# The first norm postponed behind three chunks, and one modulation piece moved, in a three-layer fp32 transformer kernel

## The reference

```python
def rmsnorm(x, g):
    y = xf * lax.rsqrt(jnp.mean(xf * xf, axis=-1, keepdims=True) + EPS) * g
h = rmsnorm(x, attn_pre_norm[l])
proj = h @ w_in[l]
...
qm = rmsnorm(c_q, q_latent_norm) @ w_uq       # c_q, c_kv, k_rope, keys, queries, values: columns of proj
kv = rmsnorm(c_kv, kv_latent_norm) @ w_ukv
```

## Time and profile before

| | us |
|---|---|
| median of 3 runs (range) | 1070.65 (1069.55 to 1073.02) |
| the profiled execution | 1071.52 |
| its span in the profile | 1069.7 |
| PE busy in the span | 1038.4 (97%) |
| DVE, ACT, POOL busy | 809.5, 589.0, 153.1 |
| granted TensorE clock, mean | 0.993 of 2.4 GHz |

### The profile page before, as it was taken

One profiled execution on the slowest core, in us unless ns is written; L12 is line 12 of the kernel. 1 busy time (PEld: TensorE's weight loads), 2 busy tenths in 40 slices (PEclk: granted clock), 3 DMA queues, 4 the chain that ended last, 5 costly groups with the idle time before them and its releaser, 6 DMA issues.

```text
span 1069.7 us, 20330 instructions
## 1 busy us (share of the span) xinstructions
PE 1038.4 (97%) x7901; PEld 986.4 (92%) x7901; DVE 809.5 (76%) x1392; ACT 589.0 (55%) x1015; POOL 153.1 (14%) x162
## 2 busy tenths in 40 slices
PE   7999999999999999999999999999999999999997
PEld 6987798999888997899999999988899999999997
DVE  5867689999997987588999788885558567675453
ACT  6686467666536675675444445533466456544442
POOL 0000033333201200023111011200000113111010
PEclk8999999999999999999999999999999999999999
DMA  9642245777695443257998788454343536774540
GB/s 365 242 158 80 80 150 201 291 287 261 257 397 233 161 154 120 89 196 281 373 350 326 279 318 305 161 193 159 119 138 140 210 143 215 251 301 137 169 166 39
DMA packets 33684, 227.25 MB, mean 212 GB/s; under 512 B 3747, under 2 KB 4044, under 8 KB 9932
## 3 DMA queue, kind: packets, MB, share of 16 engines
q1 hardware_dynamic: 33164, 223.63, 56.6%
q0 software_dynamic: 448, 2.63, 0.6%
HBM read 225.19 MB, written 2.63 MB: 213 GB/s over the span
## 4 chain that ended last, share of the span: by engine, by line
PE 72%; DVE 18%; ACT 5%; issue 3%; DMA 1%; DVEq 0%; POOL 0%; ACTq 0%; SPq 0%
PE psum L1385 17%; PE psum L1387 17%; PE psum L1386 17%; DVE w_lo L2091 7%; DVE arena L2195 4%; PE psum L1750 3%; PE psum L1752 3%; PE psum L1751 3%; PE psum L1450 2%; PE psum L1453 2%; PE psum L1452 2%; ACT w_hi L762 2%; DVE arena L2348 1%; DVE h_lo L2356 1%; DVE hid_lo L2176 1%
## 5 line engine op out<-in xcount | busy, mean ns | idle before, releaser
L2091 DVE TENSOR_TENSOR w_lo<-raw,w_hi 128x1024 fp32r<-128x1024 f32 (+1 forms) x342 | 390.9, 1165 | 155.0 <-ACT w_hi L762 147.8
L762 ACT ACTIVATE w_hi<-raw 128x1024 fp32r<-128x1024 f32 (+1 forms) x342 | 335.7, 997 | 217.1 <-PE psum L1387 161.0
L1385 PE MATMUL psum<-h_hi,w_hi 128*128 128x256 f32 (+1 forms) x1144 | 327.8, 287 | 10.2 <-DVE w_lo L2091 4.1
L1386 PE MATMUL psum<-h_lo,w_hi 128*128 128x256 f32 (+1 forms) x1144 | 322.2, 282 | 0.0
L1387 PE MATMUL psum<-h_hi,w_lo 128*128 128x256 f32 (+1 forms) x1144 | 320.9, 280 | 0.0
L1385 PE MATMUL psum<-hid_hi,w_hi 128*128 128x256 f32 (+1 forms) x952 | 271.5, 285 | 1.8 <-DVE w_lo L2091 1.5
L1387 PE MATMUL psum<-hid_hi,w_lo 128*128 128x256 f32 (+1 forms) x952 | 269.3, 283 | 0.0
L1386 PE MATMUL psum<-hid_lo,w_hi 128*128 128x256 f32 (+1 forms) x952 | 269.2, 283 | 0.0
L1385 PEld LDWEIGHTS psum<-h_hi,w_hi 128*128 128x128 f32 x1144 | 215.3, 188 | 15.2 <-DVE w_lo L2091 6.5
L1386 PEld LDWEIGHTS psum<-h_lo,w_hi 128*128 128x128 f32 x1144 | 216.3, 189 | 0.7 <-issue 0.7
L1387 PEld LDWEIGHTS psum<-h_hi,w_lo 128*128 128x128 f32 x1144 | 216.4, 189 | 0.0
(11 more groups left out here) (266 smaller groups left out, 1183.6 us busy)
## 6 DMA issues: line engine op xcount, KB each, us to landing
arena<-in_ada SPq DMA_DIRECT2D x48, 1024.0 KB, 6.3
raw<-in_gu SPq DMA_DIRECT2D x44, 1024.0 KB, 6.4
raw<-in_ret_in SPq DMA_DIRECT2D x24, 1024.0 KB, 4.7
raw<-in_up SPq DMA_DIRECT2D x22, 1024.0 KB, 4.9
raw<-in_dn SPq DMA_DIRECT2D x32, 704.0 KB, 4.2
raw<-in_qkv SPq DMA_DIRECT2D x12, 1024.0 KB, 5.4
raw<-in_down SPq DMA_DIRECT2D x11, 1024.0 KB, 7.5
raw<-in_ret_o SPq DMA_DIRECT2D x8, 1024.0 KB, 4.8
```

Source lines behind the costliest of these rows:

```text
L762: nc.scalar.activation(w_hi[chunk % SPLIT_SLOTS][:, a:b], raw[chunk % RAW_SLOTS][:, a:b], ACT.Copy)\
L1385: nc.tensor.matmul(out, w[0], hc, start=start, stop=False, skip_group_check=True)
L1386: nc.tensor.matmul(out, w[0], lc, start=False, stop=False, skip_group_check=True)
L2091: tt(w_lo[s][:, a:b], raw[chunk % RAW_SLOTS][:, a:b], w_hi[s][:, a:b].bitcast(F32), ALU.subtract)\
```

## The change

Three things.

1. The norm is postponed for LAT0, LAT1 and KA. They multiply x times its gain (`Z_PRE`, in the unused end of `hid_hi`, `hid_lo`), made by ACT and DVE straight from x. When the three leave their banks, DVE multiplies them with 1/rms (`leave_scaled`), which ACT has copied to SBUF (`rbc_pre`). QA0 is the first chunk on the normed h, whose eight tiles are made meanwhile. The sums and the spread of the norm stand inside LAT0 and LAT1. LAT0 is ordered by output half; its weights come in two DMAs; `ident` and `onehot` are loaded behind LAT1, tab1 behind QA0. 34 fillers instead of 16 stand ahead of it, none later in the norm.
2. One modulation piece leaves w_in (at QA0) and goes to up's 21st chunk (number 20), where pieces 19, 20 and 21 now follow each other.
3. The rounding of the latents stands behind the first scores and exponentials, the split of the values (ROWS1) ahead of both, and QA0's bank is emptied before the rounding.

On PE, the head of the program before; `busy` is the filler, `tra`/`sco` banks show as psum.

```diff
 ADA_PIECES = 24
-ADA_STEPS = [("w_in", 10, lambda c: int(c in (KA, QA0))), ("up", 22, lambda c: int(c >= 7 and c % 2)),
+ADA_STEPS = [("w_in", 10, lambda c: int(c == KA)), ("up", 22, lambda c: int(c >= 7 and c % 2 or c == 20)),
...
+        Z_PRE = (hid_hi[:, (FT - DT) * S:], hid_lo[:, (FT - DT) * S:])
+        rbc_pre = a1["pT"][:, 0:S]
...
             for k in (0, DT // 2):
                 cut = slice(k * S, (k + DT // 2) * S)
                 sp.dma_start(x[:, cut], dram["x"][:, cut]).then_inc(x_in[2 * k // DT], 16)
-            sp.dma_start(cols[:, :], dram["cols"]).then_inc(cols_in, 16)
-            sp.dma_start(onehot, dram["onehot"]).then_inc(onehot_in, 16)
-            sp.dma_start(ident[:, :], dram["ident"]).then_inc(ident_in, 16)
+                if k == 0:
+                    sp.dma_start(cols[:, :], dram["cols"]).then_inc(cols_in, 16)
...
                     src = dram[ph.name][bass.ds(step.n(lambda c: c * P), P), 0:n]
+                    if chunk == 0:
+                        sp.dma_start(raw[0][:, 0:n // 2], src[:, 0:n // 2]).then_inc(first_in, 16)
+                        sp.dma_start(raw[0][:, n // 2:n], src[:, n // 2:n]).then_inc(raw_in[0], 16)
+                        return
                     sp.dma_start(raw[slot][:, 0:n], src).then_inc(raw_in[slot], 16)
...
                     load(step)
                     if ph.name == "w_in" and step.j == 1:
+                        sp.dma_start(ident[:, :], dram["ident"]).then_inc(ident_in, 16)
+                        sp.dma_start(onehot, dram["onehot"]).then_inc(onehot_in, 16)
                         sp.dma_start(cond_silu, dram["cond"]).then_inc(cond_in, 16)
-                    if ph.name == "w_in" and step.j == 2:
+                    if ph.name == "w_in" and step.j == 3:
                         sp.dma_start(arena[:, TAB1_AT:TAB1_AT + dram["tab1"].shape[1]], dram["tab1"]).then_inc(tab1_in, 16)
...
-                act.wait_ge(raw_in[chunk % RAW_SLOTS], at(lambda k: 16 * (k // RAW_SLOTS + 1)))
+                if chunk or ahead != 0:
+                    act.wait_ge(raw_in[chunk % RAW_SLOTS], at(lambda k: 16 * (k // RAW_SLOTS + 1)))
                 for half, (a, b) in enumerate(of.halves(c)):
                     if ahead in (0, 1) and half != ahead:
                         continue
+                    if chunk == 0 and half == 0:
+                        act.wait_ge(first_in, 16)
...
-            for k in range(0, DT, 2):
+            act.wait_ge(cols_in, 16)
+            for k in range(DT):
                 if k % 4 == 0:
                     act.wait_ge(x_in[k // 4], 16)
+                cut = slice(k * S, (k + 1) * S)
+                nc.scalar.activation(Z_PRE[0][:, cut], x[:, cut], ACT.Identity, scale=col("pre", k)).then_inc(pre_hi, 1)
+                if k == 5:
+                    hi(0, ahead=0)
+            hi(0, ahead=1)
+            for k in range(0, DT, 2):
                 square(PRE, k, 2)
+            hi(LAT1)
             act.wait_ge(band_ps, 1)
             nc.scalar.activation(band, tra[0][0:8, 0:BAND], ACT.Copy).then_inc(band_ready, 1)
-            warm_root(PRE)
-            hi(0)
-            root(PRE)
-            round_h(PRE)
-            hi(LAT1)
             act.wait_ge(cond_in, 16)
             nc.scalar.activation(cond_silu, cond_silu, ACT.Silu).then_inc(cond_ready, 1)
+            root(PRE)
+            hi(KA)
+            act.wait_ge(rbc_ready, nth(PRE))
+            nc.scalar.activation(rbc_pre, spread_bank(PRE, 0), ACT.Copy).then_inc(pre_rbc, 1)
+            for k in range(DT):
+                round_tile(PRE, k)
+                if k in (1, 2):
+                    hi(QA0, ahead=k - 1)
+                if k == 3:
+                    act.wait_ge(lin_free[0], 1)
+                    act.wait_ge(lin_free[1], 1)
+                    square(LATENT, 0, 3)
+                if k == 6:
+                    root(LATENT)
+                    hi(ROWS0)
...
-            leave_features(LAT0, a1["lat"][:, 0:512])
-            hi(KA)
-            act.wait_ge(half_done, 2 * (LAT1 + 1))
-            nc.scalar.activation(a1["kr"], lin[1][:, S:2 * S], ACT.Copy)
-            leave(nc.scalar.activation(a1["lat"][:, 512:768], lin[1][:, 0:S], ACT.Copy), UNIT_OF[LAT1])
-            act.wait_ge(lin_free[0], 1)
-            act.wait_ge(lin_free[1], 1)
-            square(LATENT, 0, 3)
-            hi(QA0)
-            leave_features(KA, a1["ka"])
-            root(LATENT)
-            hi(ROWS0)
             nc.scalar.activation(warm[:, LATENT:LATENT + 1], ones[:, 0:1], ACT.Exp)
-            round_h(LATENT)
             leave_features(QA0, a1["qa"][:, 0:512], qscale)
             hi(ROWS1)
             exp_pair(0)
+            round_h(LATENT)
...
             hi(MLA)
             act.wait_ge(v_rows, 1)
+            act.wait_ge(h_tiles, tiles_before(GROUP))
             leave_rows(0)
...
             pe.wait_ge(busy_ready, 1)
-            keep_busy(16)
+            keep_busy(34)
             pe.wait_ge(cols_in, 16)
-            pe.wait_ge(onehot_in, 16)
-            nc.tensor.matmul(tra[0][0:8, 0:BAND], col("rel", 0, 8, BUCKETS + 1), onehot, start=True, stop=True).then_inc(band_ps, 1)
             pe.wait_ge(ones_filled, 1)
-            norm(PRE, 0, 8, 4)
+            def bias_band():
+                pe.wait_ge(onehot_in, 16)
+                nc.tensor.matmul(tra[0][0:8, 0:BAND], col("rel", 0, 8, BUCKETS + 1), onehot, start=True, stop=True).then_inc(band_ps, 1)
...
-                if first_tiles is not None:
+                if first_tiles is not None and by_tile:
                     order.sort(key=lambda o: o[1])
...
             ph = PH["w_in"]
-            features(ph, LAT0, bank_free(0), 2, DT, first_tiles=(h_tiles, 0))
-            features(ph, LAT1, bank_free(1), 2, DT)
+            features(ph, LAT0, bank_free(0), 2, DT, Z_PRE, first_tiles=(pre_tiles, 0), hooks={9: bias_band, 14: lambda: sums(PRE)}, by_tile=False)
+            features(ph, LAT1, bank_free(1), 2, DT, Z_PRE, hooks={8: lambda: spread(PRE)})
...
-            features(ph, KA, bank_free(2), 1, DT, hooks={4: rotate_keys})
+            features(ph, KA, bank_free(2), 1, DT, Z_PRE, hooks={4: rotate_keys})
             sums(LATENT)
-            features(ph, QA0, bank_free(3), 2, DT, hooks={11: lambda: spread(LATENT)})
+            features(ph, QA0, bank_free(3), 2, DT, first_tiles=(h_tiles, 0), hooks={11: lambda: spread(LATENT)})
...
             dve.wait_ge(cols_in, 16)
-            dve.wait_ge(ident_in, 16)
             dve.wait_ge(x_in[0], 16)
-            dve.wait_ge(x_in[1], 16)
+            for k in range(DT):
+                if k == 4:
+                    dve.wait_ge(x_in[1], 16)
+                cut = slice(k * S, (k + 1) * S)
+                dve.wait_ge(pre_hi, k + 1)
+                stt(Z_PRE[1][:, cut], x[:, cut], col("pre", k), Z_PRE[0][:, cut].bitcast(F32), ALU.mult, ALU.subtract).then_inc(pre_tiles, 1)
+                if k == 5:
+                    lo(0, ahead=0)
+            lo(0, ahead=1)
...
-            norm_h(PRE, lambda: lo(0))
+            lo(LAT1)
+            dve.wait_ge(ident_in, 16)
+            rstd(PRE)
+            lo(KA)
+            dve.wait_ge(cond_ready, 1)
+            pieces("w_in", Step(KA))
...
-            lo(LAT1)
-            lo(KA)
-            dve.wait_ge(cond_ready, 1)
-            pieces("w_in", Step(KA))
-            lo(QA0)
-            rstd(LATENT)
+            def leave_scaled(c, *todo):
+                dve.wait_ge(half_done, 2 * (c + 1))
+                for to, at in todo:
+                    n = to.shape[1] // S
+                    ins = tt(v3(to, n), v3(lin[UNIT_OF[c] % 2][:, at:at + n * S], n), over(rbc_pre, n), ALU.mult)
+                leave(ins, UNIT_OF[c])
+            dve.wait_ge(pre_rbc, 1)
+            leave_scaled(LAT0, (a1["lat"][:, 0:512], 0))
+            def scale_pre(k):
+                cut = slice(k * S, (k + 1) * S)
+                stt(e0["y"][:, cut], x[:, cut], col("pre", k), rbc_pre, ALU.mult, ALU.mult).then_inc(t_ready, 1)
+            scale_pre(0)
+            for k in range(DT):
+                if k + 1 < DT:
+                    scale_pre(k + 1)
+                cut = slice(k * S, (k + 1) * S)
+                dve.wait_ge(hh_ready, k + 1)
+                tt(hl[:, cut], e0["y"][:, cut], hh[:, cut].bitcast(F32), ALU.subtract).then_inc(h_tiles, 1)
+                if k == 1:
+                    leave_scaled(LAT1, (a1["lat"][:, 512:768], 0), (a1["kr"], S))
+                if k in (2, 3):
+                    lo(QA0, ahead=k - 2)
+                if k == 4:
+                    leave_scaled(KA, (a1["ka"], 0))
+                if k == 5:
+                    rstd(LATENT)
             lo(ROWS0)
             dve.wait_ge(tab1_in, 16)
             rotary(0, a1["kr"], a1["cos"], a1["sin"], 1)
+            lo(ROWS1)
+            dve.wait_ge(bias_in, 16)
+            score_pair(0)
             tiles_of(LATENT)
-            pieces("w_in", Step(QA0))
-            dve.wait_ge(bias_in, 16)
```

(2 more changed lines are left out.)

5 lines of the change are left out of this document (3 added, 2 removed).

## The result

The changed kernel took **1075.52 us** (median of 14 runs, 1072.60 to 1078.34), the kernel before 1072.99 (14 runs, 1069.55 to 1074.29): ratio **1.0027, 95% interval 1.0017 to 1.0037**. Forecast were 1069.0 and 1066.0 to 1072.4. So it is slower, by 2.5 us (the medians) to 2.9 us (the ratio), where 1.6 us of gain were forecast; only rival 1 had that size, by a mechanism that the trace does not show. The profiled execution took 1073.82 us, its span is 1071.8 (before 1071.52 and 1069.7).

What follows compares the result with a forecast made beforehand. PE was taken as full almost everywhere, so only its waits could be won. Start -3.5 and end of up +1.9 gave -1.6 on the profiled 1071.52: 1069.9, less 0.87 for the median, 1069.0 us; range 1066.0 to 1072.4.

Steps and rivals of the forecast that it cites:

- rival 1: End of up: down's four loads share the rings, chunk 0 lands at 276.3; net +2.7, 1073.4 us; chance 0.09.
- the first half of LAT0's weights lands at 8.5: Start: landing reckoned at the transfers' early rate; PE to start LAT0 at 11.0 instead of 17.14.
- If LAT0 runs at 1.2 GHz: Start: a low clock in LAT0 takes up to 4.6 us more, all but 1.9 hidden; none was counted.
- the band copy until 15.8: Start, ACT's list: the band copy follows LAT1's halves (15.4), ahead of Silu and its table, until 18.1.
- VectorE's list of 16.1 us as the bound: Start: DVE's queue binds from 20.9, eighth tile of h at 37.0; gain at the start 3.5 us.
- stood in DVE's shadow before: w_in: the piece that left (2.5 us of DVE, 1 MB of DMA) brings nothing of its own.
- SyncE's queue at the end of up: Piece 21's load waits for piece 19; down's first three chunks queue behind it, 12 us later.
- Its price, 1.9 us: Down's start: PE waits for the last taps from 279.3 to 281.2, 1.9 us; bounds 0.8 and 3.0.
- (2): End of up: the load is hidden, the piece costs 0 to 0.8 us; net -3.1, 1067.5 us; chance 0.12.
- (3): Start: DVE is quicker, gain 5 us; net -3.1, 1067.5 us; chance 0.09.
- (4): Start: the bias lands at 44.4, wanted at 41.8; 2.6 us lost, net +1.0, 1071.7 us; chance 0.09.
- (5): Start: a switch of ACT's tables costs twice its row, root 2.6 us later; net +1.0, 1071.7 us; chance 0.04.

Runs made afterwards that it cites:

- columns last: Changed kernel with its extra piece at up's chunk 8, plus the columns' transfer moved behind both halves of x; one profile, shift at 62 us -1.55.
- 52 fillers: Changed kernel with its extra piece at up's chunk 8, plus 52 fillers instead of 34; one profile, shift at 62 us -2.57.
- copied last: Changed kernel with its extra piece at up's chunk 8, plus ScalarE's band copy moved behind the root; one profile, shift at 62 us -1.55.
- the clock kept up and the band first: Changed kernel with extra piece at down's chunk 5, band's matmul and copy early, 52 fillers; ratio to before 0.9983, shift at 62 us -2.76.
- band first: Changed kernel with extra piece at up's chunk 8, band's matmul ahead of LAT0 and its copy ahead of the squares; ratio to before 0.9985.
- the piece alone: Kernel before with one edit: the piece that stood at QA0 is done at up's chunk 20; ratio to before 1.0044.
- load behind again: Second profile of the changed kernel with piece 21's load moved behind down's chunks 0 to 2; shift at 338 us +1.79.
- both pieces early with 52 fillers: The both pieces early kernel with 52 fillers instead of 34; ratio to before 1.0021.
- piece at chunk 8: Changed kernel with the extra piece at up's chunk 8 instead of 20; ratio to before 1.0005.
- both pieces early: Changed kernel with band's matmul and copy early, first piece ahead of the norm's mean, second where the first stood, eight in up; ratio to before 1.0017.

## Why the prediction was wrong, step by step

PE's large waits stood where the forecast had them, at both places; three terms of the sum were wrong. A lower clock behind an idle PE was put at nothing, twice: 1.5 us at the start and 1.7 at the end of `up`. The loads at the start delayed the root by 1.4 us, and the wait at `down` was 3.3 us and not 1.9.

- *Loads at the start* ("the first half of LAT0's weights lands at 8.5"): it landed at 10.05. x's second half kept ScalarE waiting until 8.77. This step is 1.6 us late: LAT0 at 12.62, not 11.0. It is half of why the root was late (1.4 of 2.9 us). I had divided bytes by 0.41 MB/us; with the columns between the halves of x the rate from 5 to 10 us was 344 GB/s, with the columns last 398.
- *"If LAT0 runs at 1.2 GHz ... I take none of it"*: **this is the choice that failed.** The clock did fall, behind an idle time of 3.97 us, and LAT0 took 1.5 us longer for it (7.5 us from its start to the sums against 6.0 with 52 fillers), near the 1.9 us that I had worked out as a bound and then put at nothing. It was not hidden, since LAT0's slow part delays the band's product inside it, for which ScalarE waits ahead of the root, and not only LAT1's end, which I had looked at. That is the other half.
- *"the band copy until 15.8"*: I had set it by ScalarE's own list, and forgot that it waits for a matmul behind nine of LAT0's blocks. It stood at 18.36 to 18.84. At full clock the wait is not there (52 fillers), so this miss and the one above are one and the same 1.54 us. Shown by three runs: copied first, copied last, or with PE quicker, the root comes 0.9 to 1.4 us earlier.
- *VectorE's list of 16.1 us as the bound*: right. From KA's split at 23.95 to the eighth tile of h it ran 15.9 us with one gap of 0.27, and PE's waits of 0.75 and 1.10 us were where I had put 1.0 and 1.3; the two small ones in QA0 did not come. It started 3 us later than forecast, and that is the whole of the missing gain: 3.5 forecast, 0.5 seen. With the clock kept up and the band first 2.8 were reached. What is left there is argued, not tested: the later loads and Sqrt's table, then the last step before the root (20.23).
- *The piece in w_in "stood in DVE's shadow before"*: nearly. Taken away from the kernel before, the shift at 62 us is -0.67 in one trace and +0.25 in another. Of these -0.21 and +0.40 stand already at the 5th rounding, by earlier or later loads, so the piece itself was worth some 0.5 and 0.15 us.
- *SyncE's queue at the end of up*: the mechanism was right. Loads at 252.01 and 263.33, down's chunk 0 landing at 271.42 (forecast 272.0), one wait of PE for L2439 in down's first chunk. That the landing fits so well is in part luck: the load left at 263.71, 1.4 us earlier than the 265.1 by which I had reckoned, and took 7.7 us instead of 6.9.
- *Its price, 1.9 us*: mis-sized. The taps ended at 281.67 (forecast 281.2; VectorE was half a microsecond ahead of my list until piece 21, which took 3.7 us and not 2.6), PE was there at 278.7 and not 279.3 (it was ahead of before), so it waited 3.04, and 0.25 for `w_lo` before; and **the wait took the clock with it, 1.7 us**, which I had put at nothing. My upper bound of 3.0 just covers the wait, and not its price. Nothing gave it back by 435 us: +3.93 at 338 and there.
- *Rivals*: down's chunks landed neither together (1) nor in time (2); VectorE was not quicker than its list (3); in the changed kernel nothing waited for the bias (4); the table switches (5) were as the row said.
- *The median as the profiled time less 0.87*: in 14 runs the median of before was 1072.99, not 1070.65 as in the first three. The level of my forecast was 2.3 us too low by that alone; the ratio, which is not touched by it, is 1.0027 where 0.9985 was forecast.

## What to carry to other kernels

A wait of the engine that is full costs its length and, where the granted clock falls behind it, more: 1.7 us here, in three of four traces with a wait of 1.6 to 3.0 us at that place. Price each new wait with the clock, and look at what the slowed work releases. When an item moves along a fixed order, check three queues for it: the engine's that does the work, the one that issues its load (what stands behind that load?), and the transfers' own room (which is argued here, not shown). To learn what one part of a change is worth, compare two kernels that differ in it alone, at a place next to it; the start looked like 0.5 us against the kernel before and like nothing against the kernel without the piece. A filler count is worth a test by itself whenever the first useful matmul moves.

## What the runs showed of the hardware

At a granted clock of 1.00, and with PE busy without a gap, the number of matmuls in a window still differs between executions and changes within one. Two windows, 600 to 640 and 960 to 1040 us, of the kernel before, the changed kernel and the piece alone:

```profile
600.00:640.00 40.00, 40.00 (x335) 40.00 (x335) 34.33 (x57) 18.72 (x29) 3.53 (x3) 1.00 0.86 319
960.00:1040.00 80.00, 80.00 (x679) 80.00 (x678) 39.27 (x48) 35.76 (x54) 8.71 (x11) 1.00 0.51 170
```

```profile
600.00:640.00 40.00, 40.00 (x340) 40.00 (x339) 33.71 (x56) 20.25 (x32) 2.57 (x3) 1.00 0.82 307
960.00:1040.00 80.00, 80.00 (x679) 80.00 (x678) 38.83 (x48) 36.05 (x54) 9.12 (x11) 1.00 0.48 163
```

```profile
600.00:640.00 40.00, 40.00 (x340) 40.00 (x339) 32.68 (x53) 19.45 (x30) 2.57 (x3) 1.00 0.80 305
960.00:1040.00 80.00, 80.00 (x669) 80.00 (x668) 37.97 (x47) 35.55 (x53) 8.09 (x10) 1.00 0.49 162
```

335 against 340, and 679 against 669: about 1.5%, in either direction, for the same instructions. It is not a matter of records that a trace lacks, since ScalarE's roundings move with it: the shift of the piece alone goes from 4.12 at 931 us to 5.99 at 1049, that of the changed kernel stays at 2.13 from 959 on, after it had gone from 3.92 to 2.82 between 532 and 676. Such stretches make up most of the 1.8 us that the changed kernel won behind 530 us and the 2 us that the piece alone lost behind 900, each nearly as much as this change. Its cause I don't know. So a difference of spans of two traces is no measure of a change of 0.2%; the shift at a place next to the edit is, and for the total a dozen runs each. The second such thing is the clock: at 94 us most traces, that of the kernel before too, show a stretch below 1.00 behind the heads' waits. Three did not (band first, load behind again, both pieces early with 52 fillers), and there the shift moves down by 1.5 us (-2.15 to -3.61 between 62 and 178 us with the band first); in two (piece at chunk 8, both pieces early) it was about twice as long, and the shift moves up by 1.4 to 1.6. So 1.5 us of the -1.56 at 338 us of the band first are luck of that execution.
